# A two-block transformer kernel on one core: another order of its buffers in SBUF

## The reference

```python
def first_block(x, ...):
    u = rms_norm(h, ln_mix_pre)
    hq, hf, hi, hg, aq, ak, av = split(u @ w_in)          # 2048 -> 7 x 1024
    o_rec = hgrn2_mixer(hq, hf, hi, hg, ...)               # 8 heads of 128
    o_att = dilated_attention_mixer(aq, ak, av)            # 8 heads of 128
    h = h + rms_norm(concat([o_rec, o_att]) @ w_out, ln_mix_post)
    y = conv_gated_mlp(rms_norm(h, ln_ffn_pre), w_up, conv_w, conv_b, w_down)  # 2048 -> 2*5632 -> 2048
    h = h + rms_norm(y, ln_ffn_post)
    return h + (p @ w_pe) * sigmoid(h @ w_pg)

def second_block(x, mem, ...):
    h = rmsnorm(x, norm_g)
    cv_a, cv_b, cv_gate, fq, fk, fv, f_logit, fox_gate, mq, mem_gate = split(h @ w_in)
    y_conv = (silu(layernorm(causal_conv31(cv_a * sigmoid(cv_b)))) @ w_conv_pw) * silu(cv_gate)
    y_fox = fox_attention(fq, fk, fv, log_sigmoid(f_logit + b_f)) * silu(fox_gate)
    mk, mv = split(rmsnorm(mem, mem_norm_g) @ w_mem_kv)
    y_mem = memory_attention(mq, mk, mv) * silu(mem_gate)
    return rmsnorm(x + concat([y_conv, y_fox, y_mem]) @ w_out, final_g)
```

## Time and profile before

| | |
|---|---|
| median of three runs | 1806.44 us |
| lowest and highest run | 1804.89 and 1806.96 us |
| the profiled execution, its own time | 1807.98 us |
| its span, first to last instruction | 1806.2 us |
| mean granted clock of TensorE | 0.996 |
| instructions | 29904 |
| read from the chip's memory, over the span | 323.85 MB, 180 GB/s |

### The profile page before, as it was taken

One profiled execution on the slowest core, in us unless ns is written; L12 is line 12 of the kernel. 1 busy time (PEld: TensorE's weight loads), 2 busy tenths in 40 slices (PEclk: granted clock), 3 DMA queues, 4 the chain that ended last, 5 costly groups with the idle time before them and its releaser, 6 DMA issues.

```text
span 1806.2 us, 29904 instructions
## 1 busy us (share of the span) xinstructions
PE 1778.2 (98%) x10326; PEld 1557.8 (86%) x10326; DVE 1258.7 (70%) x1560; ACT 944.1 (52%) x1253; POOL 641.4 (36%) x631
## 2 busy tenths in 40 slices
PE   9999999999999999999999999999999999999997
PEld 7888888888878888888888888888888888888886
DVE  6676676666577887777777644444887688888754
ACT  5454444445366555555555533334655577665532
POOL 4714444434734333211111322222253155561032
PEclk9989999999999999999999999999999999999999
DMA  8434444445555555555555455556555444444453
GB/s 312 159 133 164 163 163 165 163 163 210 186 207 190 186 186 187 191 194 192 188 186 186 169 189 190 192 190 202 177 186 197 163 165 169 173 168 147 181 186 116
DMA packets 50429, 326.57 MB, mean 181 GB/s; under 512 B 5712, under 2 KB 6352, under 8 KB 17744
## 3 DMA queue, kind: packets, MB, share of 16 engines
q1 hardware_dynamic: 49808, 323.86, 50.5%
q10 hardware_dynamic: 576, 2.11, 0.3%
HBM read 323.85 MB, written 2.10 MB: 180 GB/s over the span
## 4 chain that ended last, share of the span: by engine, by line
PE 86%; DVE 5%; issue 4%; ACT 2%; DMA 1%; POOL 1%; SPq 0%; ACTq 0%; DVEq 0%; POOLq 0%
PE ps L1757 54%; PE ps L1758 27%; PE ps_lev L1832 2%; DVE wlo L942 1%; DMA stage<-in_w_a 1%; ACT whi L440 1%; POOL mixed L1677 1%; PE ps_sc L1796 1%; PE ps_t L1786 1%; PE ps_t L2080 0%; DVE x_in L1236 0%; DVE fs L1488 0%; PE bank_a L1801 0%; DVE tmp L948 0%; DVE y L1233 0%
## 5 line engine op out<-in xcount | busy, mean ns | idle before, releaser
L1757 PE MATMUL ps<-act_a,whi 128*128 128x512 f32 x3072 | 1079.3, 395 | 2.8 <-DVE wlo L942 1.4
L942 DVE TENSOR_TENSOR wlo<-stage,whi 128x2048 fp32r<-128x2048 f32 (+1 forms) x316 | 707.9, 2241 | 250.6 <-ACT whi L440 246.5
L1758 PE MATMUL ps<-act_a,wlo 128*128 128x256 f32 x3072 | 859.7, 280 | 0.0
L1757 PEld LDWEIGHTS ps<-act_a,whi 128*128 128x128 f32 x3072 | 578.0, 188 | 130.0 <-DVE wlo L942 2.0
L440 ACT ACTIVATE whi<-stage 128x2048 fp32r<-128x2048 f32 (+1 forms) x316 | 569.4, 1802 | 124.9 <-DMA stage<-in_w_down 104.3
L1758 PEld LDWEIGHTS ps<-act_a,wlo 128*128 128x128 f32 x3072 | 578.1, 188 | 0.3
L1757 PE MATMUL ps<-big,whi 128*128 128x512 f32 x1584 | 551.8, 393 | 4.0 <-DVE big L1342 2.6
L1758 PE MATMUL ps<-big,wlo 128*128 128x256 f32 x1584 | 442.7, 280 | 0.0
L1757 PEld LDWEIGHTS ps<-big,whi 128*128 128x128 f32 x1584 | 297.3, 188 | 71.3 <-issue 2.9
L447 ACT ACTIVATE small<-ps 128x256 f32<-128x256 f32 x247 | 94.1, 381 | 475.1 <-PE ps L1758 475.0
L1758 PEld LDWEIGHTS ps<-big,wlo 128*128 128x128 f32 x1584 | 297.4, 188 | 0.1
(11 more groups left out here) (354 smaller groups left out, 1329.7 us busy)
## 6 DMA issues: line engine op xcount, KB each, us to landing
stage<-in_w_a SPq DMA_DIRECT2D x166, 1024.0 KB, 4.8
stage<-in_w_b SPq DMA_DIRECT2D x87, 1024.0 KB, 4.8
stage<-in_w_down SPq DMA_DIRECT2D x64, 704.0 KB, 4.1
stage<-in_w_a SPq DMA_DIRECT2D x8, 256.0 KB, 9.7
mem_raw<-in_memT SPq DMA_DIRECT2D x1, 2048.0 KB, 9.3
mem_again<-in_memT SPq DMA_DIRECT2D x1, 2048.0 KB, 9.2
x_in<-in_xT ACTq DMA_DIRECT2D x3, 512.0 KB, 8.9
x_in<-in_xT SPq DMA_DIRECT2D x3, 512.0 KB, 7.4
```

What stands on the lines that cost most here:

```text
L942: dve.tensor_tensor(wlo[:, slot, part], stage[:, slot, part], whi[:, slot, part].bitcast(F32), ALU.subtract).then_inc(w_lo, 1)
L1757: pe.matmul(dst, whi[:, slot, c * P:(c + 1) * P], act, start=start, stop=False)
L1758: return pe.matmul(dst[:, T:2 * T], wlo[:, slot, c * P:(c + 1) * P], act[:, 0:T], start=False, stop=stop)
```

## The change

Only the start addresses of the buffers differ; no instruction is added, removed or put elsewhere, and every buffer keeps its size. The small constants `ident`, `cols`, `bfox`, `dummy` and `eps` come first; then the address is rounded up to a multiple of 2048; then `stage`, `whi`, `act_a` and `big` follow, each of which is a multiple of 2048 long; then `x_in` and the rest.

```diff
+        KB = 1024
+        ident = sb("ident", [P, P])
+        cols = sb("cols", [P, 32])
+        bfox = sb("bfox", [FOX_ROWS, 1])
+        dummy = sb("dummy", [P, 2])
+        eps = sb("eps", [P, 1])
+        at[0] = (at[0] + 2 * KB - 1) // (2 * KB) * (2 * KB)
         stage_at = at[0]
         stage = sb("stage", [P, NS, BW])
         wlo = over("wlo", stage_at, 0, [P, NS, BW], F32R)
         whi = sb("whi", [P, NS, BW], F32R)
+        a_at = at[0]
+        act_a = sb("act_a", [P, KT, 2 * T], F32R)
+        big_at = at[0]
+        big = sb("big", [P, FT, 2 * T], F32R)
         h_at = at[0]
         x_in = sb("x_in", [P, KT + KT * T])
...
         vec = sb("vec", [P, N_VEC])
-        ident = sb("ident", [P, P])
         ones = sb("ones", [P, P])
-        bfox = sb("bfox", [FOX_ROWS, 1])
         mkv = sb("mkv", [P, HEADS, T])
         small = sb("small", [P, 2, T])
         tmp = sb("tmp", [P, 2, T])
         rstd = sb("rstd", [P, T])
         acc = sb("acc", [P, T])
-        cols = sb("cols", [P, 32])
-        dummy = sb("dummy", [P, 2])
-        eps = sb("eps", [P, 1])
...
         at[0] = conv_at + 4128 + 1024
-        a_at = at[0]
-        act_a = sb("act_a", [P, KT, 2 * T], F32R)
-        big_at = at[0]
-        big = sb("big", [P, FT, 2 * T], F32R)
-        KB = 1024
```

## The result

The changed kernel takes 1820.26 us (median of 5 runs, 1816.34 to 1823.65), the kernel before 1806.44 us (median of 5, 1804.89 to 1808.31). The ratio is 1.0075, with a 95% interval of 1.0064 to 1.0086: slower by 14 us, where no change was forecast and no more than 1812 us allowed for. The runs of the new kernel also spread over 7.3 us, those of the old one over 3.4 us.

What follows compares the result with a forecast made beforehand. The prediction took TensorE's stream of float32r matmul pairs, 89% of the span, to bound the kernel. Its four address terms, 0 + 0 + 0 + 0, left the median at 1806.4 us, range 1800 to 1812 us.

Steps and rivals of the forecast that it cites:

- What bounds the kernel: TensorE's stream of float32r matmul pairs: 4656 pairs at 0.3469 us, 1615 us, 89% of the span.
- The moving operand of the pair: act_a and big, moved from 1824 to 0 modulo 2048 and read by the matmul pairs: put at zero cost.
- The bounds of 112 us either way: Moving-operand limits: 0.024 us a pair lost down to the nearest rows, or that excess paid twice.
- The stationary operand: Weights whi and wlo, moved from 1152 to 0 modulo 2048: zero cost, bounded by 12 us either way.
- Operands of the other engines: ScalarE, VectorE and GpSimd buffers losing or gaining a multiple of 64: zero, at most 0.4 us either sign.
- writes of the DMA queue: Loads into stage and x_in, moved from 128 to 0 modulo 256: zero, at most 2.3 us either way.
- Rival B: Moving and weight reads of TensorE meet at equal places, every fourth pair paying 0.024 us: 1834 us, chance 0.06.
- four differences between the streams cost the same: Evidence against that meeting of reads: sixteen up-projection pairs across four weight-cell placements averaged 0.3469 us.
- Rival A: Better-aligned float32r reads make the pair up to 0.024 us faster: 1694 us in full, 1750 at half; chance 0.12.
- Rival C: Lower-clock stretch at 98 to 108 us vanishes (1801.7 us, chance 0.04) or a second comes (1811.1 us, 0.05).
- The sum: Over the whole kernel, four address effects of zero each, leaving the earlier median of 1806.4 us unchanged.

Runs made afterwards that it cites:

- weights_32: Changed kernel with only the weight buffers stage and whi 32 bytes earlier, act_a and big left at multiples of 2048: 1806.59 us, ratio 0.9997.
- both_32: Changed kernel with stage, whi, act_a, big and everything behind them 32 bytes earlier, distances among them kept: 1816.32 us, ratio 1.0054.
- before_moving_96: Kernel before with 96 unused bytes ahead of act_a, moving operand and weights then equal modulo 128: 1818.12 us, ratio 1.0078.
- the fifth set: Four kernels with further distances between moving operand and weight buffers, compared with the kernel before: medians from 1808.05 to 1833.41 us.
- 32, 32: Moving operand 32 bytes behind stage and whi modulo 128, as in the kernel before; that kernel without its 256-column low-part matmuls: 1547.57 us.
- 64, 64: Kernel before with 32 bytes added ahead of act_a, distances 64 to stage and whi modulo 128: 1833.49 us; without low-part matmuls 1548.23 us.
- 0, 0: Moving operand 0 bytes behind stage and whi modulo 128, as in the changed kernel against the kernel before: 1820.26 us.

## Why the prediction was wrong

**What bounds the kernel** was read rightly: the pair is 89% of the span, the other engines and the loads are ahead, and the whole change came as a price of the pair.

**The moving operand of the pair** is the step that failed. It was put at zero, and it cost 3.5 ns a pair, 16.3 us, with 6.6 ns as the full price of a slow pattern. "I take zero: it is what both comparisons inside the trace read" rested on two comparisons that could not see it. Plain float32 shows no reaction: 0.217 us before and 0.216 and 0.217 us after. Neither of its two streams alternates between two weight tiles either, so the format and the missing alternation are not told apart. And in the earlier trace rows the two placements are 1024 bytes apart, so their difference to the weights is the same modulo 128. They do vary the crossing of 2 KB, and that it costs nothing still stands: the crossing is gone in the changed kernel and in `weights_32`, and the latter takes 0.9997 of the time before. The bounds of 112 us either way held the measured 16 us, the slow one only because it was drawn as wide as the fast one, from no row; the likeliest value inside them was taken as if the question had been measured. I had even written that a float32r read at 0 modulo 64 was missing from the trace, and gave it no width of its own in the range.

**The stationary operand.** Zero for the weights' own placement is right (`both_32` and `before_moving_96` agree with the changed kernel from other addresses). Its evidence was blind in the same way: cells of 512 bytes go through four placements modulo 2048, all alike modulo 128.

**Operands of the other engines** and **writes of the DMA queue** at zero were right: 423, 425, 371 and 367 ns against the earlier trace rows, 4.8 us to landing as in the earlier trace rows, 12.23 us against the 12.33 of the earlier trace rows. The prediction's estimate by the page "DMA: Bandwidth & Descriptors" of the Trainium skill (section "How a descriptor splits into AXI transactions") was 0.3 us less for the better start address; 0.1 us is what the one load in the chain shows, too little to tell.

**Rival B**, with 0.06, named the right kind of thing, two reads of TensorE that meet at equal places, and 1834 us, which is what the constant slow patterns take (1833.4 to 1833.8 us). It was wrong on the place: no period of four cells appeared, all pairs of a stretch pay, and the measure is a difference modulo 128, not equality modulo 2048. Its counter-evidence, "four differences between the streams cost the same", was the step that pushed it down, and those four are one. **Rival A** fell: no placement took the excess away. The 325 ns for a pair, worked out from the formula for a single gap on the page "TensorE: Matmul & The Clock Gate" of the Trainium skill (section "Back-to-back issue gap"), were not reached anywhere; the quickest stretch took 343.

**Rival C, the clock.** "It is the same in all of them" was wrong. The stretch at 1.2 GHz behind that wait (3.7 to 4.1 us) lasted 10.2 us in nine of the eighteen profiled executions that keep the low parts, 6.8 in six and 3.4 in three, with no order by placement; between the ends lie 3.4 us of time. The kernel before varies too: its mean granted clock goes from 0.995 to 0.998 in the sixteen runs beside the fifth set. A stretch of 10.2 us at half speed costs 5.1 us, where the prediction had 4.7. It widens the spread of every kernel here and explains none of the 14 us.

**The sum** was right in form; the part given back, 3.5 us of 16.3, it had no term for.

## What to carry to other kernels

When float32r matmuls alternate between two weight tiles, treat the distance between the moving buffer and each weight buffer, modulo 128 bytes, as a parameter: try several before settling on a layout, on the stream of matmuls that you have (pairs and triples did not order them alike here), and don't assume that round addresses are good ones. A comparison inside one trace counts only if it varies the quantity that could matter; list what all compared placements have in common before concluding "no difference". And read a mean over all pairs, stage by stage and in more than one execution, since a single block can show the old price in a kernel that has become slower.

## What the runs showed of the hardware

- The same pair of float32r matmuls (512 and 256 columns) takes 343, 346.7 or 353.3 ns from start to start over long stretches in kernels that differ by addresses alone.
- At some placements one program settles differently from execution to execution: 1813.64 to 1828.49 us in seven runs of `before_moving_96`, against 1804.89 to 1809.20 us in twenty runs of the kernel before, each on one chip. Two profiled executions of the changed kernel (1820.78 and 1811.21 us) differed in pattern mainly in one stretch of 410 us.
- A 512-column stream on one weight buffer takes 234.4 ns at 32, 32 and 233.4 at 64, 64, where the pair takes 346.7 and 353.2; plain float32 (0.216 to 0.217 us for 256 columns) shows no effect.
- Float32r matmuls of 256 columns, two on one weight buffer and one on the other in turn, take 119.7 to 119.9 ns each at 0, 0 and 116.6 to 118.3 at 32, 32.
- The stretch at 1.2 GHz after the same wait (3.7 to 4.1 us) lasted 3.4, 6.8 or 10.2 us; the changed kernel alone showed 10.2 in one execution and 3.4 in the next.
